# Eight ring places instead of ten, and a quarter of the query weights kept on chip for both blocks

## The reference

```python
for layer in range(DEPTH):                       # DEPTH = 2
    h = rms_norm(x, norm_mix[layer])
    z = h @ w_in[layer]                          # 1024 x 2564
    ...                                          # three kinds of attention and an S5 state space
    mixed = jnp.concatenate([fox_o, dil_o, diff_o, s5_o], axis=-1)
    x = x + mixed @ w_out[layer]
    x = x + peer(rms_norm(x, norm_ffn[layer]), peer_wq[layer], peer_keys[layer],
                 peer_u[layer], peer_v[layer])

# peer, for each chunk of 128 tokens
q = (xc @ wq).reshape(c, PEER_HEADS, 2, PEER_QDIM // 2)   # wq: 1024 x 2048
sc = jnp.einsum('thpd,hpkd->thpk', q, keys)
...                                              # top 16 pairs of keys a head: 8 x 16 = 128 ids a token
act = gelu(jnp.einsum('td,thkd->thk', xc, u_tab[ids])) * gate
return jnp.einsum('thk,thkd->td', act, v_tab[ids])
```

## Time and profile before

| | |
|---|---|
| median of the runs | 1626.78 us |
| the profiled execution | 1617.68 us (span 1615.9 us) |
| PE busy | 1419.2 us, 88% |
| DVE busy | 1131.7 us, 70% |
| ACT busy | 459.6 us, 28% |
| POOL busy | 586.3 us, 36% |
| moved by DMA | 635.23 MB, mean 393 GB/s |

### The profile page before, as it was taken

One profiled execution on the slowest core, in us unless ns is written; L12 is line 12 of the kernel. 1 busy time (PEld: TensorE's weight loads), 2 busy tenths in 40 slices (PEclk: granted clock), 3 DMA queues, 4 the chain that ended last, 5 costly groups with the idle time before them and its releaser, 6 DMA issues.

```text
span 1615.9 us, 15418 instructions
## 1 busy us (share of the span) xinstructions
PE 1419.2 (88%) x4754; PEld 766.0 (47%) x4754; DVE 1131.7 (70%) x2798; ACT 459.6 (28%) x1124; POOL 586.3 (36%) x525
## 2 busy tenths in 40 slices
PE   7898879998988798887998799999998977778688
PEld 4657335554564344444466344555456523333233
DVE  5867998864556787885456888887456886765554
ACT  3532234342211224432221233444222222121112
POOL 1003325543423244453432433545432433333332
PEclk9999989999999999999999999999999989899989
DMA  9459899999999999999999999999999899999997
GB/s 365 156 196 412 356 389 370 405 372 422 417 407 362 424 421 417 420 421 418 421 414 374 412 421 415 421 421 401 420 417 412 354 423 421 421 421 421 422 422 319
DMA packets 103134, 635.23 MB, mean 393 GB/s; under 512 B 9569, under 2 KB 10721, under 8 KB 34958
## 3 DMA queue, kind: packets, MB, share of 16 engines
q0 software_dynamic: 74144, 537.97, 80.8%
q1 hardware_dynamic: 28910, 96.29, 15.3%
HBM read 631.58 MB, written 2.64 MB: 392 GB/s over the span
## 4 chain that ended last, share of the span: by engine, by line
PE 47%; DMA 26%; DVE 17%; issue 6%; ACT 2%; another core or an unknown queue 1%; POOL 1%; SPq 0%; DVEq 0%; POOLq 0%; ACTq 0%
PE ps L1570 28%; DMA ring<-table_uv,ids 24%; PE ps L1537 7%; DVE ring L1207 5%; PE ps L1347 3%; PE ps L1515 3%; DMA W<-peer_wq 2%; ACT acts L726 1%; ACT diag L749 1%; PE ps L1417 1%; DVE W L985 1%; PE ps L1553 1%; DVE W L1182 1%; DVE W L1180 1%
## 5 line engine op out<-in xcount | busy, mean ns | idle before, releaser
L1570 PE MATMUL ps<-ring,diag 128*128 128x512 f32 x2016 | 937.3, 620 | 147.7 <-ACT diag L749 138.2
L1623 POOL DMA_INDIRECT ring<-table_uv,ids x512 | 581.0, 1135 | 991.1 <-PE ps L1570 856.2
L1570 PEld LDWEIGHTS ps<-ring,diag 128*128 128x128 f32 x2016 | 392.8, 199 | 643.1 <-issue 630.1
L1207 DVE CUSTOM_DVE_ANT_0 ring<-ring,h 128x1024 f32<-128x1024 f32 x384 | 457.2, 1223 | 189.2 <-DMA ring<-table_uv,ids 187.3
L726 ACT ACTIVATE acts<-dots,small 128x4 f32<-128x4 f32 x126 | 37.4, 297 | 849.5 <-DVE dots L1207 824.2
L1207 DVE CUSTOM_DVE_ANT_0 ring<-ring,ps 128x1024 f32<-128x1024 f32 x120 | 145.0, 1220 | 99.1 <-DMA ring<-table_uv,ids 98.7
L749 ACT ACTIVATE diag<-cst,weights 128x128 f32<-128x128 f32 x504 | 161.0, 390 | 29.0 <-DVE weights L1216 29.0
L1537 PE MATMUL ps<-hT,W 128*128 128x128 f32 x960 | 114.8, 282 | 16.6 <-DMA W<-peer_wq 16.6
L1537 PEld LDWEIGHTS ps<-hT,W 128*128 128x128 f32 x960 | 113.3, 199 | 19.1 <-issue 19.1
L1347 PE MATMUL ps<-W,hT 128*128 128x512 f32 (+2 forms) x256 | 95.2, 527 | 2.7 <-DVE hT L859 2.7
L1347 PEld LDWEIGHTS ps<-W,hT 128*128 128x128 f32 x256 | 48.5, 190 | 52.0 <-issue 47.4
(11 more groups left out here) (304 smaller groups left out, 1144.7 us busy)
## 6 DMA issues: line engine op xcount, KB each, us to landing
W<-peer_wq SPq DMA_DIRECT2D x13, 2048.0 KB, 28.9
W<-w_in SPq DMA_DIRECT2D x16, 1282.0 KB, 10.0
W<-w_out SPq DMA_DIRECT2D x8, 2048.0 KB, 18.2
ring<-table_uv,ids POOLq DMA_INDIRECT x512, 13.2
W<-w_in SPq DMA_DIRECT2D x8, 898.0 KB, 9.3
W<-w_in SPq DMA_DIRECT2D x4, 1024.0 KB, 11.5
ring<-w_in SPq DMA_DIRECT2D x2, 1544.0 KB, 18.5
ring<-w_in SPq DMA_DIRECT2D x2, 1536.0 KB, 21.8
```

The costliest lines, as they stand in the source:

```text
L1207: v.tensor_tensor_reduce(ring_u[:, r, :], ring_u[:, r, :], tokens, 1.0, 0.0, ALU.mult, ALU.add, dots[:, s:s + 1]).then_inc(dots_done, 1)
L1570: mm = pe.matmul(ps[:, c, :], diag[:, s, :], ring_v[:, r, c * 512:(c + 1) * 512], start=(k == 0), stop=(k == SLOTS - 1), skip_group_check= ...
L1623: gp.indirect_dma_start(ring[:, t % RING, :], None, table_uv, bass.IndirectOffsetOnAxis(ap=ids[:, b, k:k + 1], axis=0)).then_inc(pair_in[t ...
```

## The change

The ring has eight places. The 16 KB a partition that this frees hold quarter 1 of the query weights (`wq_kept`), loaded once a layer, right behind quarter 0. So quarters 2 and 3 have a slot each, and quarter 3 no longer waits for the use of quarter 1. In the second layer the wait ahead of quarter 0 is now for one more query of the pass before (the reader of the kept quarter). The wait of gather 8 for quarter 1 goes, since that no longer lies in the ring; gather 8 now waits for a place.

```diff
-RING = 10
+RING = 8
...
+        wq_kept = sb("wq_kept", [P, KC, 512])
...
-        wq_early = pool[:, 16384:20480].rearrange("p (k n) -> p k n", k=KC)
 
         def wq_at(n, i):
             if i == 0:
                 return wq_first
-            return wq_early if n == 0 and i == 1 else wq_slots[i % 2]
+            return wq_kept if i == 1 else wq_slots[i % 2]
...
                 if b == 0:
                     if n:
-                        sp.wait_ge(qT_ps, 4 * n - 3)
+                        sp.wait_ge(qT_ps, 4 * n - 2)
                     sp.dma_start(wq_first, wq_quarters[0]).then_inc(wq_first_in, 16)
+                    sp.dma_start(wq_kept[:, :, :], wq_quarters[1]).then_inc(wq_kept_in, 16)
                 if n == 0:
-                    sp.dma_start(wq_early, wq_quarters[1]).then_inc(wq_early_in, 16)
                     sp.wait_ge(lines_out, 16)
...
                 sp.wait_ge(wo_ps, n + 1)
-                if n:
-                    sp.dma_start(wq_at(n, 1), wq_quarters[1]).then_inc(wq_in[1], 16)
-                else:
+                if n == 0:
                     sp.wait_ge(s5_sin, 4)
                 sp.dma_start(wq_at(n, 2), wq_quarters[2]).then_inc(wq_in[0], 16)
-                if n:
-                    sp.wait_ge(qT_ps, 4 * n + 2)
                 sp.dma_start(wq_at(n, 3), wq_quarters[3]).then_inc(wq_in[1], 16)
...
                 if q == 0:
                     pe.wait_ge(wq_first_in, 16 * (n // NB + 1))
-                elif q == 2:
-                    pe.wait_ge(wq_in[0], 16 * (n + 1))
-                elif n == 0 and q == 1:
-                    pe.wait_ge(wq_early_in, 16)
+                elif q == 1:
+                    pe.wait_ge(wq_kept_in, 16 * (n // NB + 1))
                 else:
-                    pe.wait_ge(wq_in[1], 16 * (2 * n + q // 2))
+                    pe.wait_ge(wq_in[q % 2], 16 * (n + 1))
...
                         elif t == 4:
                             gp.wait_ge(z_ps, 8)
                             gp.wait_ge(s5_out, 16 * (DEPTH - 1))
-                        elif t == 8:
-                            gp.wait_ge(qT_ps, 2)
```

More of the change, by code:

```diff
@@ L344, in trunk @@
         wq_in = [sem(f"wq_in{k}") for k in range(2)]
-        wq_first_in, wq_early_in, wout_low_load = sem("wq_first_in"), sem("wq_early_in"), sem("wout_low_load")
+        wq_first_in, wq_kept_in, wout_low_load = sem("wq_first_in"), sem("wq_kept_in"), sem("wout_low_load")
         row_load, s5_load, glu_load, ffn_load, wout_load, keys_load = (
```

## The result

The changed kernel takes 1681.07 us (median of four runs, 1666.59 to 1682.62) against 1625.5 for the kernel before on the same chip: + 55.6 us. The ratio with its 95% interval is 1.0316, 1.0292 to 1.0339; it is estimated from all of the runs and so counts the one of 1666.59, which is some 14 us under the other three (the medians alone give 1.034). The forecast was 1630.7 with a range up to 1645. So the change costs 55.6 us where the sum had + 3.9. The profiled execution took 1680.35 us.

The account below looks back on a forecast made before the run. The kernel was taken as DMA-bound, PE behind by a few us. Query stretches -4.0, -3.5, -2.0, moved load +5.4, last pass +5, elsewhere +3 sum to +3.9; from the median 1626.78 this gives 1630.7 us, range 1617 to 1645.

Parts of the forecast that it names:

- What bounds the kernel: Whole kernel: DMA-bound, with PE behind by a few us in three query stretches; 11.3 us of idle DMA there.
- the opening loses nothing: Opening: bound by DVE, so gathers 8 and 9 going out some 20 us later cost nothing.
- Part 1 and 2: Query stretches: two loads fewer, third queries' waits vanish; -4.0, -3.5 and -2.0 us in passes 1, 2 and 3.
- Part 3: Pass 2: quarter 1's load moves behind quarter 0, where gathers are the limit; +5.4 us, bounds 0 and 5.4.
- Part 4, elsewhere: Shorter ring outside the last pass: DVE's lateness to most dots absorbs part of the loss; +3 us, bounds 0 and 8.
- part 2: Passes 1 to 3: PE's waits for weights go, worth 7.7, 7.4 and 6.3 us before the lost gather lead.
- Part 4, the last pass: Shorter ring: margin 1.8 us in an even cycle, lost only after DVE's searches; +5 us, bounds 2 and 11.
- rival B: DMA-bound stretches: issue to landing over 7.8 us, 0.6 us lost per pair of groups; +18, 1645 us, chance 0.23.
- A: Shorter ring: low latency leaves room enough and more of the lead survives; -8, or 1619 us, chance 0.22.
- C: Query loads: quarter 2 still comes too late, so the change doesn't do what it says; 1638 us, chance 0.05.

Follow-up runs that it names:

- e3: Kernel before, ten places, with the changed kernel's loads; second query of passes 1 to 3 reads the first's buffer, so not usable: 1609.5 us, 0.9898.
- e12: Kernel before with a window of eight gathers only where one pass turns into the next: 1633.88 us, 1.0058.
- e13: Kernel before with a window of eight only for gathers 16 to 103 of passes 0 to 2, the mixing stretches: 1666.66 us, 1.0258.
- e8: Kernel before with a window of eight gathers in the last pass alone: 1645.62 us, 1.0121.
- e4: Changed kernel, releasing places gather by gather from the second group of the last pass on: 1667.07 us, 1.0253.
- e5: Changed kernel plus three small unread products on PE behind each group's rows of v in the last pass: 1668.16 us, 1.0251.
- e6: Changed kernel without the searches of heads 2 to 7 in passes 1 to 3, ids copied from heads 0 and 1: 1679.73 us, 1.0337.
- e1: Kernel before, layout and loads unchanged, only POOL's wait shortened to a window of eight gathers: 1688.44 us, 1.0366.
- e2: Kernel before, layout and loads unchanged, only POOL's wait shortened to a window of nine gathers: 1642.63 us, 1.0092.
- e10: Changed kernel with both the small PE products in the last pass and the searches of heads 2 to 7 left out: 1655.94 us, 1.0221.
- e9: Kernel before, ten places, with the small unread PE products in the last pass: 1622.21 us, 1.0014.

## Why the prediction was wrong

**What bounds the kernel, and that the opening loses nothing:** right in the main. At group 8 the changed kernel is level with the ten-place kernels. One reading was off: the share is under 1.02 not "in just three stretches" but in the last pass too, 0.98. PE's idle time and slow matmuls were in that stretch already.

**Part 1 and 2, the loads and PE's waits:** the three waits went as forecast, and the queries run at 7.31 us. The query stretches gained 2.4, 3.1 and 4.5 us (groups 26 to 30, 60 to 64, 90 to 94), 10.0 against the forecast's 9.5. That the sums agree is luck: by stretch the forecast had 4.0, 3.5 and 2.0, and it had meant what is left after the loss of the lead, which comes only behind these stretches. With ten places they gain 9.3, 6.8 and 8.2. Behind them the changed kernel falls back 7.4 us by group 40, 6.2 by group 68 and 2.4 by group 96, where e3 loses at most 0.8. I had let the w_in loads fill that gap, and they don't. So part 2 ends at + 6.0 instead of - 9.5. With the short window at the turns alone (e12) the whole costs + 9.

**Part 3, the moved load:** right. e3 loses 5.3 us between groups 40 and 44 (- 7.8 to - 2.5) against 5.4 forecast; with eight places it is 3.2, inside the bounds of 0 to 5.4; that part of it rides in gaps is likely, but not shown.

**Part 4, elsewhere: this is the step that failed first.** It said + 3, bounds 0 and 8. With the short window in the mixing stretches alone e13 measures + 42, and the changed kernel loses 26.0 us there (sum below). I had measured the margin in one place, the even cycle of the last pass (19.9 us for eight gathers, 12.0 until the release, 6.0 to land), and argued for the other passes by DVE's cover. The rows to look at were in the same trace. Here is the kernel before in the mixing stretch of pass 0, timelines of DVE, PE and POOL:

```profile
388.58 1.23 DVE L1207 CUSTOM_DVE_ANT_0 ring<-ring,h 128x1024 f32<-128x1024 f32 x1 [0.39 <-DMA ring<-table_uv,ids]
...
397.98 3.60 PE L1515 MATMUL ps<-W,hT 128*128 128x512 f32 x8
...
401.41 3.60 PE L1570 MATMUL ps<-ring,diag 128*128 128x512 f32 x8
...
403.57 1.98 POOL L1623 DMA_INDIRECT ring<-table_uv,ids  x1 [4.24 <-PE ps L1570]
```

The plan puts a piece of the mixing part, here 3.60 us of the output product, between a group's weights and its rows of v. The release comes 15.0 us after the first dot, not 12.0, and the first dot of the group after the next starts 19.9 us after it, as in the last pass: 15.0 + 6.0 is over that.

How often this happens is less clear. By the last pass's figures 16 of the 66 groups of the kernel before in the mixing stretches release too late (later than 13.9 us after their first dot), by 28 us in all. That is close to the 26.0 us lost, but by chance. In 14 of the 16 the eight gathers take not 19.9 but 22.8 to 29.8 us, so that a later release would do; held against its own time from dot to dot, with the same 6.0 us to land, only 2 groups are short, by 1.6 us in all. By pass the count gives 8.4, 10.2 and 9.9 us, while the changed kernel loses 11.7, 1.8 and 12.5. DVE's cover, which the forecast relied on, is there for most of them: in 11 of the 16 the first dot of the group after the next hardly waits for its gather (0.04 us or less).

What the traces do show is that the DMA ran short of gathers there. Over the three stretches (groups 8 to 26, 44 to 60, 68 to 90) the changed kernel takes 26 us longer than e8; slow gather packets (over 0.4 us) make 15 of these (21.0 us over 16 engines against 6.1), and 9 more are time without a packet, averaged over the engines. PE's groups of rows of v are also slow there more often, 13 of 66 against 6. Which releases began it, PE's piece of the mixing part, a slow group or the lead lost before, no experiment has told apart; e4, e5 and e6 are about the last pass. So that the term was far too small is shown, and why stays in part open.

**Part 4, the last pass:** + 5 forecast (2 to 11), + 21 to 22 measured. The margin of 1.8 us in an even cycle was right: e5, with eight places, runs such cycles. Timelines of DVE, PE and POOL:

```profile
1509.91 1.22 DVE L1203 CUSTOM_DVE_ANT_0 ring<-ring,ps 128x1024 f32<-128x1024 f32 x1 [0.72 <-DMA ring<-table_uv,ids]
...
1519.70 7.10 PE L1564 MATMUL ps<-ring,diag 128*128 128x512 f32 x16 [0.69 <-ACT diag L745]
...
1521.93 0.94 POOL L1618 DMA_INDIRECT ring<-table_uv,ids  x1 [3.85 <-PE ps L1564]
...
1529.79 1.22 DVE L1203 CUSTOM_DVE_ANT_0 ring<-ring,ps 128x1024 f32<-128x1024 f32 x1 [0.73 <-DMA ring<-table_uv,ids]
```

19.88 us for eight gathers, 7.86 of them from issue to dot, and no gap. (The prediction's 1520.47 is a slip for the row's 1520.51; nothing hangs on it.) So rival B's mechanism (issue to landing too long in the even cycle) is not what happened, though it had the sign and 19 us. What the step left out is what PE does after it has waited, although part 2 had priced just that for the queries (9.24 us instead of 7.31). The changed kernel's last pass, PE,

```profile
1554.96 8.78 PE L1564 MATMUL ps<-ring,diag 128*128 128x512 f32 x16 [2.83 <-ACT diag L745]
1564.88 7.10 PE L1564 MATMUL ps<-ring,diag 128*128 128x512 f32 x16 [1.15 <-ACT diag L745]
1575.80 8.60 PE L1564 MATMUL ps<-ring,diag 128*128 128x512 f32 x16 [3.81 <-ACT diag L745]
```

and POOL's first gathers after the second and the third of these groups:

```profile
1567.11 0.94 POOL L1615 DMA_INDIRECT ring<-table_uv,ids  x1 [2.16 <-PE ps L1564]
...
1580.02 0.94 POOL L1615 DMA_INDIRECT ring<-table_uv,ids  x1 [6.83 <-PE ps L1564]
```

After 1.15 us of idle time the release comes 2.2 us after PE's start (1567.11 - 1564.88); after 3.81 it comes 4.2 us after (1580.02 - 1575.80), and that takes the margin of 1.8. Then a gather is late, so the dots, the weights and PE are late, PE idles longer, and its next matmuls start slowly: the loss feeds itself. Of the 30 groups of four in the changed kernel's last pass, the 9 with the longest idle time before them (4.0 to 5.1 us) took 8.6 to 10.1 us, the 12 with the shortest (0 to 1.9) 7.1 us each, at a granted clock of 0.89 for the pass, that is, partly on the 1.2 GHz level. The same stands in the trace of before (a group of 9.72 us after 3.83 idle at 1531.29, but also one of 8.80 after 1.92), with ten places to cover it. It is even in the rows that the prediction used: the release that is 3.4 us late at 1335.18 was put down to DVE's "ids" alone, but PE had started at 1331.45, after 4.74 us of idle time, and the issue came 3.7 us later and not 2.2. So 1.5 of the 3.4 us were slow matmuls.

The Trainium skill, page TensorE: Matmul & The Clock Gate, section HAM oscillation, describes the same kind of loop: waits for DMA between short bursts of matmuls put the array back on its slow clock again and again. The traces here agree in kind, with the difference that PE waits for ACT's diagonal matrices, and these for a gather. With the waits filled the clock of the pass is 0.99 instead of 0.89 and 11 to 13 us are gained (e5).

The searches, which I had priced at + 5, are the other source: gathers 384 to 447 lose 14.2 us, and 5.0 with the searches away. Seven late groups were counted, each with its own lateness only; what a late group does to the next ones, by PE's idle time, was put at nothing.

**The rivals:** A (the ring has room enough) is out. C is out: the change does what it says. B had the right sign, but the measured time lies far above its 1645 too.

The sum by the measured terms, from the table: mixing stretches + 26.0 (11.7, 1.8 and 12.5), query stretches - 10.0, what follows them + 16.0 (7.4, 6.2 and 2.4), moved load + 3.2, and + 20.7 from group 96 to group 127 (+ 22.1 to the end of the execution), makes + 55.9 (57.3 to the end). The median moved by 55.6. Against the forecast the mixing stretches are 23 us over, the last pass 16, part 2 with what follows it 15.5, and the moved load 2 under.

## What to carry to other kernels

Before a ring is shortened, run the shorter window first: one changed wait (e1, e2), with no new layout, gave 62 and 16 us. Reading the trace gives less. One even cycle tells the margin, not the price; and a count of late releases names the stretches to look at, but its sum means nothing unless each group is held against its own cycle, and here it gave no price even so. Where the margin is a few us, one late release makes TensorE idle, its next matmuls are slow, and the next release is late as well; one place fewer cost 16 us here, two four times that. Of the 22 us that the last pass lost, releasing in smaller pieces bought back 18 (e4), and work that keeps TensorE busy 11 (e5).

## What was not expected of the hardware

**A queue that runs nearly dry goes on with slow packets, and the busy share hides it.** A gather's packet of 8 KB takes 0.31 us. In the last 124 gathers of the kernel before, 10 of 15872 took over 0.4 us. In the changed kernel 705 did, half of these over 0.56 and up to 2.19 us. Their extra time over 16 engines is 16 us, most of the 21 lost there; in e10 it is 2.3, with a window of seven 28. The queue is not idle for long, it restarts slowly, for instance at 1581.5, 1.5 us after the late issue above:

```profile
1581.50:1582.50 1.00, 1.00 (x3) 0.38 (x2) 0.65 (x2) 0.00 (x0) 0.70 (x1) 1.00 0.87 188
```

A DMA share of 0.87 moved 188 GB/s. So a full-looking DMA row must be read with the GB/s beside it.

**Added matmuls made a kernel faster** (e5, 11 to 13 us, 0.7 to 0.8% of the whole), and the same matmuls did nothing with ten places (e9). Idle time of an engine that isn't the bottleneck was not free here: it set the clock of the work that released the buffers.
